# A one-core hybrid attention layer: x normed before it is split, instead of a factor on every projection

## The chip, the cores and the metric

One Trainium2 chip, one of its cores. The metric is device microseconds (us) of one execution of the kernel. All data are float32; matrix products run on float32 values that are first split into a high part `hi` and a remainder `lo`.

## What is computed

The reference, cut to what matters here (S = 256 tokens, width 2048, 256 memory tokens):

```python
h = rmsnorm(x, norm_g)                 # x * rsqrt(mean(x*x)) * norm_g
z = h @ w_in                           # (256, 6144), split into the next line
q_a, k_a, v_a, g_a, u_p, g_p, q_m, g_m = jnp.split(z, IN_OFFSETS, axis=-1)
y_a = causal_attention(q_a, k_a, v_a) * silu(g_a)      # 8 heads x 128
y_p = multiscale_pool(u_p, w_pool, pool_scale) * silu(g_p)
mk, mv = jnp.split(rmsnorm(mem, mem_norm_g) @ w_mem_kv, 2, axis=-1)
y_m = memory_attention(q_m, mk, mv) * silu(g_m)        # 4 heads x 128
y = jnp.concatenate([y_a, y_p, y_m], axis=-1) @ w_out
return rmsnorm(x + y, final_norm_g)
```

## The kernel before

All weights together are 18 **groups** of 512 columns, and a group is 8 **pieces** of 2 x 128 rows (512 KB), so that `n` runs over 144 pieces and `g, a = divmod(n, 8)`. The groups are, in order: MK (n 0 to 7) and MV (8 to 15), the memory's keys and values; Q0 (16 to 23), Q1, K0, K1, V0, V1, GA0, GA1, U, GP, QM, GM, which are projections of x; and four output groups. Every engine runs its own program over the same `n`, and semaphores join them:

- **SP** sends the weights into 8 buffers `w_raw`. In its loop at L276 it waits until piece a of MK has been split, sends piece a of MV (L278) and then two of the 16 slices of x turned (`x_t_raw`, L279). After it `w_pool` and the weights of `w_in` (L285) follow in one queue.
- **ACT** (ScalarE) makes `hi` of piece n+4 in step n (`split_hi`, L516 to L524). That waits for piece n to be used up by TensorE and for piece n+4 to have landed.
- **DVE** (VectorE) makes `lo = raw - hi` of the same piece (`split_lo`, L696).
- **PE** (TensorE) multiplies piece n once `lo` of it is there (L473). Groups MK, Q, K, GA, U, GP, QM, GM go through `rows_are_features` (the wide `hi` product and a half-wide `lo` product), MV, V0, V1 and the output groups through `rows_are_tokens` (three wide products, L387 to L389).
- Results leave PSUM at a == 7: ACT copies one half into `part_b` (L618), DVE adds the other in `evacuate` (L755); V0 and V1 leave with a factor (L746).

The norm of x: x turned is multiplied by `norm_g` alone while it is split, by `x_to_hi` on ACT (L552) and `x_to_lo` on DVE (L724), in steps n = 10 to 17 (`X_FIRST` = 10). The factor 1/rms comes in later. x by rows (`rows`, 2 x 1 MB) is sent from ACT's queue at n == 8 (L630) and squared in steps 16 to 19 (`square_rows`, L535, by the table `SQUARE_STEPS`, L61). At n == 20 DVE takes the mean (`mean_square`, L701), GpSimd raises it to the power -1/2 (L322), and DVE puts it on diagonals (`spread_diag`, L732). After piece n == 22 PE spreads these over all partitions (`spread_rstd`, L348, called at L485), and DVE copies the result to `x_rstd` (L833). All groups of x except Q0, Q1 and QM are then multiplied by `x_rstd` as they leave (L759) or by the token's factor (L746), and the scores' factor is applied in `scale_max` (L762) and in the exponential's scale (L570). In each step of DVE's program the order is: evacuation, `x_rstd`, `split_lo`, the part of x, the mean (L825 to L847). In ACT's: `part_b`, `split_hi`, squares, the DMAs of `rows`, x (L612 to L634).

Of the kernel before, what the change touches and what calls it, by code (L numbers as in the profile page):

```python
# [21 lines left out]
F32 = mybir.dt.float32  # L22
F32R = mybir.dt.float32r
ALU = mybir.AluOpType
ACT = mybir.ActivationFunctionType
AX = mybir.AxisListType

P = 128
D = 2048
S = 256  # L30
# [5 lines left out]
TH = S // P  # L36
# [21 lines left out]
JOBS = (V1, GA0, GM)  # L58
FACTOR = {Q0: SCALE, Q1: SCALE, QM: SCALE, GA0: 0.5, GA1: 0.5, GP: 0.5, GM: 0.5}
BRANCHES = (V1, GA0, GP, GM)  # L60
SQUARE_STEPS = {16: (0,), 17: (1,), 18: (2,), 19: (3,), 24: (4,), 25: (5,), 26: (6,), 27: (7,)}  # L61
X_FIRST = PPG + 2
X_GAIN, POOL_SCALE = 0, KT
X_MEAN, X_SPREAD = 20, 22
GATES = (GA0, GA1, GP, GM)


def build(nc, x, mem, x_t, mem_head, columns, w_in, w_mem_kv, w_pool, w_out, final_g, out):
    with ExitStack() as ctx:
# [3 lines left out]
        def sem(name):  # L73
            return ctx.enter_context(nc.semaphore(name))
# [103 lines left out]
        mk_scaled = sem("mk_scaled")  # L178
        mem_hi = sem("mem_hi")
        mem_lo = sem("mem_lo")  # L180
        x_hi = sem("x_hi")
        x_lo = sem("x_lo")
        mv_scaled = sem("mv_scaled")
# [44 lines left out]
        def bank0(g):  # L228

            return 4 * (g % 2)  # L230
# [18 lines left out]
        @block.sync  # L249
        def _(sp):  # L250
            def mem_slices(i):

                sp.dma_start(mem_raw[:, mem_columns(i)], mem_head[:, mem_columns(i)]).then_inc(mem_landed[i], 16)

            def first_half(a):

                sp.dma_start(w_raw[:, a, 0], kv_dram[0, a, :, 0]).then_inc(first_landed[a], 16)

            def second_half(a):

                sp.dma_start(w_raw[:, a, 1], kv_dram[0, a, :, 1]).then_inc(landed[a], 16)

            sp.dma_start(mem_raw[:, 0:KT + S], mem_head[:, 0:KT + S]).then_inc(mem_first_landed, 16)
            second_half(0)
            mem_slices(1)
            first_half(1)
            second_half(1)
            mem_slices(2)
            first_half(2)
            second_half(2)  # L270
            for a in range(HALVED, PPG):
                if TPP * a in MEM_CHUNKS:
                    mem_slices(MEM_CHUNKS.index(TPP * a))
                sp.dma_start(w_raw[:, a], kv_dram[0, a]).then_inc(landed[a], 16)
            sp.dma_start(cols[:, :], columns).then_inc(cols_landed, 16)
            for a in range(PPG):  # L276
                sp.wait_ge(lo_done, a + 1)
                sp.dma_start(w_raw[:, a], kv_dram[1, a]).then_inc(landed[a], 16)  # L278
                sp.dma_start(x_t_raw[:, TPP * a:TPP * (a + 1)], x_t[:, TPP * a:TPP * (a + 1)]  # L279
                             ).then_inc(x_landed[a], 16)  # L280
            sp.dma_start(wp[:, :, :], w_pool).then_inc(wp_landed, 16)
            with sp.Fori(0, OUT0 - Q0) as g:
                for a in range(PPG):
                    sp.wait_ge(lo_done, g * PPG + (PPG + a + 1))
                    sp.dma_start(w_raw[:, a], in_dram[bass.ds(g, 1), a].rearrange("g p t c -> p (g t) c")  # L285
                                 ).then_inc(landed[a], 16)
            with sp.Fori(0, GROUPS - OUT0) as g:
                for a in range(PPG):
                    sp.wait_ge(lo_done, g * PPG + ((OUT0 - 1) * PPG + a + 1))
                    sp.dma_start(w_raw[:, a], out_w_dram[bass.ds(g, 1), a].rearrange("g p t c -> p (g t) c")  # L290
                                 ).then_inc(landed[a], 16)
            for h in range(TH):
                for i in range(3):
                    c = slice(i * COLS, (i + 1) * COLS)
                    sp.wait_ge(finished_dve, 3 * h + i + 1)
                    sp.dma_start(out_dram[h, :, c], x_res[:, h, c]).then_inc(stored, 16)
                sp.wait_ge(finished_act, h + 1)
                sp.dma_start(out_dram[h, :, D - COLS:], end_scaled[:, h]).then_inc(stored, 16)
            sp.wait_ge(stored, 16 * 4 * TH)
# [215 lines left out]
        def _(act):  # L515
# [35 lines left out]

            def x_to_hi(b):  # L552

                act.wait_ge(x_landed[b], 16)
                for kt in (2 * b, 2 * b + 1):
                    m = act.activation(xT[:, kt, 0], x_t_raw[:, kt], ACT.Copy,
                                       scale=cols[:, X_GAIN + kt:X_GAIN + kt + 1])
                m.then_inc(x_hi, 1)

            def exps(g, pair):  # L560
                j = 2 * JOBS.index(g) + pair
                act.wait_ge(max_ready, j + 1)
                if j == 0:
                    act.wait_ge(mk_scaled, 1)
                for f in range(2 * pair, 2 * pair + 2):
                    for h in range(TH):
                        c, w = (h * M, M) if g == MEM_JOB else (h * P, P + h * P)
                        dst = probs_end if g == MEM_JOB else probs
                        m = act.activation(dst[:, f, c:c + w], ps[:, bank0(g + 1) + f, c:c + w], ACT.Exp,
                                           scale=rstd_in[:, 0, h:h + 1],  # L570
                                           bias=nmax[:, f, h:h + 1], accum_out=sums[:, f, h:h + 1])
                m.then_inc(exp_done, 1)

# [36 lines left out]
            for n in range(PIECES):  # L610
# [14 lines left out]
                    split_hi(m)  # L625
                for k in SQUARE_STEPS.get(n, ()):
                    square_rows(k)
                if n == PPG:
                    for h in range(TH):
                        act.dma_start(rows[:, h], x_dram[h]).then_inc(rows_landed[h], 16)  # L630
                if n == X_FIRST:
                    act.wait_ge(cols_landed, 16)
                if X_FIRST <= n < X_FIRST + PPG:
                    x_to_hi(n - X_FIRST)  # L634
                if n == 20:
# [51 lines left out]
        def _(dve):  # L687
            steps = [0]

            def settle(ins):  # L690

                steps[0] += 1
                ins.then_inc(dve_self, 1)
                dve.wait_ge(dve_self, steps[0])
# [21 lines left out]
            def mem_to_lo(kts):  # L716
                for kt in kts:
# [3 lines left out]
                                             in1=memT[:, kt, 0].bitcast(F32),  # L721
                                             op0=ALU.mult, op1=ALU.subtract).then_inc(mem_lo, 1)

            def x_to_lo(b):  # L724
                dve.wait_ge(x_hi, b + 1)
                for kt in (2 * b, 2 * b + 1):
                    m = dve.scalar_tensor_tensor(out=xT[:, kt, 1], in0=x_t_raw[:, kt],
                                                 scalar=cols[:, X_GAIN + kt:X_GAIN + kt + 1],
                                                 in1=xT[:, kt, 0].bitcast(F32), op0=ALU.mult, op1=ALU.subtract)
                m.then_inc(x_lo, 1)  # L730

            def spread_diag(i):  # L732
                dve.wait_ge(rstd_ready, i + 1)
# [4 lines left out]
            def evacuate(g):  # L738
# [3 lines left out]
                    return  # L742
                if g in TOKENS_ON_ROWS:
                    dst = {V0: v[:, :, 0:COLS], V1: v[:, :, COLS:]}[g]
                    for h in range(TH):
                        m = dve.tensor_scalar(dst[:, h], ps[:, bank0(g) + h, :], rstd_in[:, 0, h:h + 1], None, ALU.mult)  # L746
                    m.then_inc(evacuated, 1)
                    return
                dst = {MK: mkT, QM: qmT, Q0: qT[:, 0:NF], Q1: qT[:, NF:], K0: kT[:, 0:NF], K1: kT[:, NF:],
                       U: u_pad[:, :, PAD:]}.get(g, gate)  # L750
# [1 line left out]
                if g in GATES and g != GA0:  # L752
                    dve.wait_ge(y_lo, GATES.index(g))
                hi_part = ps[:, bank0(g):bank0(g) + NF, 0:S]
                m = dve.scalar_tensor_tensor(out=dst[:, :, :], in0=hi_part, scalar=FACTOR.get(g, 1.0),  # L755
                                             in1=part_b[:, :, :], op0=ALU.mult, op1=ALU.add)
                if g not in (MK, Q0, Q1, QM):
                    settle(m)
                    m = dve.tensor_tensor(dst[:, :, :], dst[:, :, :], x_rstd[:, :, :].to_broadcast([P, NF, S]), ALU.mult)  # L759
                m.then_inc(evacuated, 1)  # L760

            def scale_max(own):  # L762

                dve.tensor_tensor(nmax[:, own, :], nmax[:, own, :], rstd_in[:, 0:1, :].to_broadcast([P, 2, TH]),
                                  ALU.mult).then_inc(max_ready, 1)

            def mask_and_max(g, pair):
                j = 2 * JOBS.index(g) + pair
# [1 line left out]
                b = bank0(g + 1) + 2 * pair  # L770
                own = slice(2 * pair, 2 * pair + 2)
                if g == MEM_JOB:
                    settle(dve.tensor_reduce(nmax[:, own, :], ps[:, b:b + 2, :].rearrange("p f (h k) -> p f h k", h=TH),
                                             AX.X, ALU.max, negate=True))
                    scale_max(own)
                    return

                diag = ps[:, b:b + 2, :].rearrange("p f (h k) -> p f h k", h=TH)[:, :, :, 0:P]
                settle(dve.tensor_tensor(diag, diag, mask[:, :].rearrange("p (f h k) -> p f h k", f=1, h=1)
                                         .to_broadcast([P, 2, TH, P]), ALU.add))  # L780
                dve.tensor_reduce(nmax[:, own, 0:1], ps[:, b:b + 2, 0:P], AX.X, ALU.max, negate=True)
                settle(dve.tensor_reduce(nmax[:, own, 1:2], ps[:, b:b + 2, P:P + S], AX.X, ALU.max, negate=True))
                scale_max(own)

            def normalise(g, pair):
                j = 2 * JOBS.index(g) + pair
# [37 lines left out]
            for n in range(PIECES):  # L824
# [13 lines left out]
                    split_lo(m)  # L838
                if n == X_FIRST:
                    dve.wait_ge(cols_landed, 16)  # L840
                if X_FIRST <= n < X_FIRST + PPG:
                    x_to_lo(n - X_FIRST)
                if n == X_MEAN:
                    mean_square(0)
# [97 lines left out]
```

## Time and profile before

| | us |
|---|---|
| median of 3 runs | 440.05 (439.99 to 440.51) |
| the profiled execution's own time | 439.82 |
| its span, first to last instruction | 437.6 |
| PE busy | 428.5 |
| DVE busy | 266.3 |
| ACT busy | 220.1 |
| GpSimd busy | 26.5 |

The span is 2.2 us shorter than the execution's time. Rows of a timeline are: start, duration, engine, line, operation, output and inputs, count, and in brackets the idle time before it with what ended it. "PE" is the matmul, "PEld" the load of its stationary operand, which overlaps. Matmul rows overlap each other, since their ends are modelled.

### The profile page before, as it was taken

How to read it: one execution, taken by the hardware profiler on the slowest of the kernel's cores; microseconds unless marked ns; L12 is line 12 of the kernel's file. 1: busy time of each engine (PE TensorE's matmuls, PEld its weight loads, DVE VectorE, ACT ScalarE, POOL GpSimd, SP SyncE). 2: the span in 40 equal slices, each digit the busy share in tenths (PEclk: the TensorE clock that was granted, in tenths of full speed). 3: DMA queues.
4: the chain of work that ended last, by engine and by line, in shares of the span. 5: the costliest groups of instructions: out<-in, count | busy, mean ns of one | idle time of the engine just before them, and what ended most of it. 6: DMA issues, size and time to landing. Idle time of an engine off the chain costs nothing.

```text
span 437.6 us, 6006 instructions
## 1 busy us (share of the span) xinstructions
PE 428.5 (98%) x2252; PEld 367.8 (84%) x2252; DVE 266.3 (61%) x293; ACT 220.1 (50%) x298; POOL 26.5 (6%) x48
## 2 busy tenths in 40 slices
PE   9999999999999999999999999999999999999992
PEld 8888888888888888888988888888888888888881
DVE  4865865545464685746466767848663674648522
ACT  6854784743444435536545444454465544357311
POOL 1000000000000020000020200010000202020200
PEclk9999999999999999999999999999999999999998
DMA  8999969655556554643629866445735256746022
GB/s 286 405 402 411 389 197 381 193 187 183 190 176 193 188 169 161 189 145 99 194 97 355 318 202 199 160 168 185 219 119 192 95 175 212 228 156 194 0 97 97
DMA packets 25657, 89.77 MB, mean 205 GB/s; under 512 B 2976, under 2 KB 3232, under 8 KB 24736
## 3 DMA queue, kind: packets, MB, share of 16 engines
q1 hardware_dynamic: 24336, 81.69, 54.9%
q10 hardware_dynamic: 1296, 7.73, 4.3%
q8 instruction: 18, 0.29, 0.3%
q14 instruction: 7, 0.06, 0.1%
HBM read 87.31 MB, written 2.10 MB: 204 GB/s over the span
## 4 chain that ended last, share of the span: by engine, by line
PE 95%; issue 2%; DVE 0%; POOL 0%; ACT 0%; POOLq 0%; DVEq 0%
PE ps L365 38%; PE ps L368 17%; PE ps L387 11%; PE ps L389 11%; PE ps L388 11%; PE ps L374 1%; PE ps L444 1%; PE ps L404 1%; PE ps L435 1%; PE ps L431 1%; PE ps L399 1%; PE ps L419 1%; PE ps L403 0%; PE ps L436 0%; PE ps L415 0%
## 5 line engine op out<-in xcount | busy, mean ns | idle before, releaser
L699 DVE TENSOR_TENSOR w_lo<-w_raw,w_hi 128x1024 fp32r<-128x1024 f32 x137 | 173.9, 1282 | 119.4 <-ACT w_hi L524 119.0
L524 ACT ACTIVATE w_hi<-w_raw 128x1024 fp32r<-128x1024 f32 x137 | 143.7, 1058 | 130.1 <-PE ps L368 74.6
L365 PE MATMUL ps<-xT,w_hi 128*128 128x512 f32 x640 | 200.6, 397 | 0.0
L368 PEld LDWEIGHTS ps<-xT,w_lo 128*128 128x128 f32 x600 | 112.7, 188 | 26.6
L368 PE MATMUL ps<-xT,w_lo 128*128 128x256 f32 x600 | 118.1, 278 | 0.0
L365 PEld LDWEIGHTS ps<-xT,w_hi 128*128 128x128 f32 x640 | 98.8, 189 | 1.3
L387 PE MATMUL ps<-w_hi,yT 128*128 128x512 f32 x112 | 43.6, 389 | 0.0
L388 PE MATMUL ps<-w_lo,yT 128*128 128x512 f32 x112 | 43.6, 389 | 0.0
L389 PE MATMUL ps<-w_hi,yT 128*128 128x512 f32 x112 | 43.6, 389 | 0.0
L387 PE MATMUL ps<-w_hi,xT 128*128 128x512 f32 x64 | 25.5, 399 | 0.0
L389 PE MATMUL ps<-w_hi,xT 128*128 128x512 f32 x64 | 25.0, 390 | 0.0
L388 PE MATMUL ps<-w_lo,xT 128*128 128x512 f32 x64 | 24.9, 389 | 0.0
L389 PEld LDWEIGHTS ps<-w_hi,yT 128*128 128x128 f32 x112 | 21.0, 188 | 4.4
L388 PEld LDWEIGHTS ps<-w_lo,yT 128*128 128x128 f32 x112 | 21.0, 188 | 4.4
L387 PEld LDWEIGHTS ps<-w_hi,yT 128*128 128x128 f32 x112 | 21.0, 188 | 4.3
L618 ACT ACTIVATE part_b<-ps 128x1024 f32<-128x1024 f32 x11 | 11.3, 1027 | 20.3 <-PE ps L368 20.3
L365 PE MATMUL ps<-memT,w_hi 128*128 128x512 f32 x64 | 20.6, 407 | 0.0
L333 POOL TENSOR_TENSOR gate<-gate,att 128x1024 f32<-128x1024 f32 x4 | 9.6, 2411 | 122.0 <-ACT part_b L666 122.0
L595 ACT ACTIVATE squares<-x_res 128x512 f32<-128x512 f32 x8 | 5.1, 633 | 22.5 <-DVE x_res L891 15.2
L389 PEld LDWEIGHTS ps<-w_hi,xT 128*128 128x128 f32 x64 | 12.0, 188 | 2.6
L388 PEld LDWEIGHTS ps<-w_lo,xT 128*128 128x128 f32 x64 | 12.0, 188 | 2.3
L387 PEld LDWEIGHTS ps<-w_hi,xT 128*128 128x128 f32 x64 | 12.0, 188 | 2.3
(129 smaller groups left out, 384.9 us busy)
## 6 DMA issues: line engine op xcount, KB each, us to landing
w_raw<-in_w_in SPq DMA_DIRECT2D x96, 512.0 KB, 4.2
w_raw<-in_w_out SPq DMA_DIRECT2D x32, 512.0 KB, 4.2
w_raw<-in_w_mem_kv SPq DMA_DIRECT2D x13, 512.0 KB, 13.1
x_t_raw<-in_x_t SPq DMA_DIRECT2D x8, 256.0 KB, 13.6
rows<-in_x ACTq DMA_DIRECT2D x2, 1024.0 KB, 10.5
rows<-in_mem ACTq DMA_DIRECT2D x2, 1024.0 KB, 9.0
x_res<-in_x ACTq DMA_DIRECT2D x2, 1024.0 KB, 8.9
mem_raw<-in_mem_head SPq DMA_DIRECT2D x3, 512.0 KB, 7.6
```

What stands on the lines that cost most here:

```text
L333: pool.tensor_tensor(gate[:, :, :], gate[:, :, :], att[:, i % 2], ALU.mult).then_inc(gate_att, 1)
L365: pe.matmul(ps[:, bank0(g) + f, :], hi[:, t, f * P:(f + 1) * P], moving[:, kt], start=(kt == 0), stop=(kt == KT - 1), skip_group_check=True)
L368: m = pe.matmul(ps[:, bank0(g) + f, 0:S], lo[:, t, f * P:(f + 1) * P], moving[:, kt, 0], start=False, stop=(kt == KT - 1), skip_group_chec ...
L374: pe.matmul(ps[:, bank0(g) + f, 0:S], lo[:, t, f * P:(f + 1) * P], moving[:, kt, 0], start=False, stop=False, skip_group_check=True)
L387: pe.matmul(acc, stationary[:, kt, 0, tok], hi[:, t, :], start=(kt == 0), stop=False)
L388: pe.matmul(acc, stationary[:, kt, 0, tok], lo[:, t, :], start=False, stop=False)
L389: m = pe.matmul(acc, stationary[:, kt, 1, tok], hi[:, t, :], start=False, stop=(kt == KT - 1))
L399: m = pe.matmul(ps[:, b, h * M:(h + 1) * M], qmT[:, f, h * P:(h + 1) * P], mkT[:, f, :], start=True, stop=True)
L524: act.activation(halves_of(n)[0], w_raw[:, n % RAW], ACT.Copy).then_inc(hi_done, 1)
L595: act.activation(squares[:, 0:c.stop - c.start], x_res[:, h, c], ACT.Square, scale=D ** -0.5, accum_out=ssq[:, h, i:i + 1]).then_inc(sq_do ...
L618: act.activation(part_b[:, :, :], ps[:, bank0(g):bank0(g) + NF, S:2 * S], ACT.Copy, scale=FACTOR.get(g, 1.0)).then_inc(part_b_ready, 1)
L699: dve.tensor_tensor(lo, w_raw[:, n % RAW], hi.bitcast(F32), ALU.subtract).then_inc(lo_done, 1)
```

## The change

x turned is multiplied in place by `norm_g` and 1/rms on DVE (`norm_x`), one step ahead of its use, and only then split: ACT copies two slices in one instruction, DVE subtracts in one. For this `x_rstd` has to be known before the split. Its mean moves from step 20 to step 10, the spreading from 22 to 12, the squares from steps 16 to 19 to steps 6 to 9, and the split of x from steps 10 to 17 to steps 13 to 20. x by rows is sent by SP, half 0 behind piece 0 of MV's weights and slices of x, half 1 behind piece 1. The factors at the exits are gone.

```diff
-SQUARE_STEPS = {16: (0,), 17: (1,), 18: (2,), 19: (3,), 24: (4,), ...}
-X_FIRST = PPG + 2
+SQUARE_STEPS = {6: (0,), 7: (1,), 8: (2,), 9: (3,), 24: (4,), ...}
+X_MEAN, X_SPREAD = PPG + 2, PPG + 4
+X_FIRST = X_SPREAD + 1
-X_MEAN, X_SPREAD = 20, 22
@@ SP, after piece a of MV and its slices of x_t
+                if a < TH:
+                    sp.dma_start(rows[:, a], x_dram[a]).then_inc(rows_landed[a], 16)
@@ ACT
             def x_to_hi(b):
-                act.wait_ge(x_landed[b], 16)
-                for kt in (2 * b, 2 * b + 1):
-                    m = act.activation(xT[:, kt, 0], x_t_raw[:, kt], ACT.Copy,
-                                       scale=cols[:, X_GAIN + kt:X_GAIN + kt + 1])
-                m.then_inc(x_hi, 1)
+                act.wait_ge(x_normed, b + 1)
+                act.activation(xT[:, 2 * b:2 * b + 2, 0], x_t_raw[:, 2 * b:2 * b + 2], ACT.Copy).then_inc(x_hi, 1)
@@ exps
-                                           scale=rstd_in[:, 0, h:h + 1],
@@ ACT's loop
-                if n == PPG:
-                    for h in range(TH):
-                        act.dma_start(rows[:, h], x_dram[h]).then_inc(rows_landed[h], 16)
-                if n == X_FIRST:
-                    act.wait_ge(cols_landed, 16)
@@ DVE
+            def norm_x(b):
+                dve.wait_ge(x_landed[b], 16)
+                for kt in (2 * b, 2 * b + 1):
+                    m = dve.scalar_tensor_tensor(out=x_t_raw[:, kt], in0=x_t_raw[:, kt],
+                                                 scalar=cols[:, X_GAIN + kt:X_GAIN + kt + 1],
+                                                 in1=x_rstd[:, 0, :], op0=ALU.mult, op1=ALU.mult)
+                m.then_inc(x_normed, 1)
             def x_to_lo(b):
+                own = slice(2 * b, 2 * b + 2)
                 dve.wait_ge(x_hi, b + 1)
-                for kt in (2 * b, 2 * b + 1):
-                    m = dve.scalar_tensor_tensor(out=xT[:, kt, 1], in0=x_t_raw[:, kt], ...)
-                m.then_inc(x_lo, 1)
+                dve.tensor_tensor(xT[:, own, 1], x_t_raw[:, own], xT[:, own, 0].bitcast(F32), ALU.subtract
+                                  ).then_inc(x_lo, 1)
@@ evacuate: V0, V1
-                    for h in range(TH):
-                        m = dve.tensor_scalar(dst[:, h], ps[:, bank0(g) + h, :], rstd_in[:, 0, h:h + 1], None, ALU.mult)
+                    dve.tensor_copy(dst, ps[:, bank0(g):bank0(g) + TH, :]).then_inc(evacuated, 1)
@@ evacuate: the others keep the scalar_tensor_tensor alone
-                if g not in (MK, Q0, Q1, QM):
-                    settle(m)
-                    m = dve.tensor_tensor(dst[:, :, :], dst[:, :, :], x_rstd[:, :, :].to_broadcast([P, NF, S]), ALU.mult)
@@ mask_and_max: scale_max and the settle ahead of it are gone
-            def scale_max(own):
-                dve.tensor_tensor(nmax[:, own, :], nmax[:, own, :], rstd_in[:, 0:1, :].to_broadcast([P, 2, TH]),
-                                  ALU.mult).then_inc(max_ready, 1)
@@ DVE's loop
                 if n == X_FIRST:
                     dve.wait_ge(cols_landed, 16)
+                    norm_x(0)
                 if X_FIRST <= n < X_FIRST + PPG:
+                    if n + 1 < X_FIRST + PPG:
+                        norm_x(n + 1 - X_FIRST)
                     x_to_lo(n - X_FIRST)
```

## Rows read from the trace of the kernel before

**Rows 1.** The page: busy time by engine, and GB/s moved in 40 slices of the span.
```profile
PE 428.5 (98%) x2252; PEld 367.8 (84%) x2252; DVE 266.3 (61%) x293; ACT 220.1 (50%) x298; POOL 26.5 (6%) x48
...
GB/s 286 405 402 411 389 197 381 193 187 183 190 176 193 188 169 161 189 145 99 194 97 355 318 202 199 160 168 185 219 119 192 95 175 212 228 156 194 0 97 97
```
**Rows 2.** Stretches: length, busy PE, PEld, DVE, ACT, POOL, granted clock, DMA share, GB/s.
```profile
6.70:429.50 422.80, 422.76 (x2230) 362.26 (x2228) 261.73 (x284) 214.94 (x289) 23.94 (x17) 1.00 0.60 207
429.60:433.20 3.60, 0.00 (x0) 0.00 (x0) 2.82 (x6) 1.45 (x3) 0.55 (x1) 1.00 0.00 0
433.40:437.60 4.20, 0.00 (x0) 0.00 (x0) 0.00 (x0) 0.00 (x0) 0.00 (x0) 0.50 0.74 239
```
**Rows 3.** The chain that ended last: shares by engine, then three of its pieces.
```profile
PE 95%; issue 2%; DVE 0%; POOL 0%; ACT 0%; POOLq 0%; DVEq 0%
...
1.00 4.63 PE ps L444 x20
5.63 1.49 PE ps L365 x4
...
51.27 0.92 PE ps L365 x4
```
**Rows 4.** Groups of DVE instructions by line and shape: busy us, mean ns, idle before.
```profile
L759 DVE TENSOR_TENSOR gate<-gate,x_rstd 128x1024 f32<-128x1024 f32 x4 | 4.9, 1226 | 0.1
...
L746 DVE TENSOR_SCALAR v<-ps,rstd_in 128x512 f32<-128x512 f32 x4 | 2.8, 746 | 2.1 <-PE ps L389 2.1
...
L709 DVE TENSOR_TENSOR w_lo<-w_raw,w_hi 128x512 fp32r<-128x512 f32 x3 | 2.1, 693 | 0.5 <-ACT w_hi L530 0.5
...
L764 DVE TENSOR_TENSOR nmax<-nmax,rstd_in 128x4 f32<-128x4 f32 x6 | 1.0, 163 | 0.2
```
**Rows 5.** SP's queue, 10 to 12.2 us: DMA issues.
```profile
10.06 0.59 SPq L278 DMA_DIRECT2D w_raw<-in_w_mem_kv  x1
...
12.17 0.68 SPq L278 DMA_DIRECT2D w_raw<-in_w_mem_kv  x1
```
**Rows 6.** DMA issues from 12.0 to 12.2 us: size, us from issue to landing.
```profile
w_raw<-in_w_mem_kv SPq DMA_DIRECT2D x1, 512.0 KB, 13.9
```
**Rows 7.** ACT's timeline, 26 to 42 us.
```profile
26.19 1.06 ACT L524 ACTIVATE w_hi<-w_raw 128x1024 fp32r<-128x1024 f32 x1 [0.89 <-PE ps L368]
28.91 1.02 ACT L618 ACTIVATE part_b<-ps 128x1024 f32<-128x1024 f32 x1 [1.67 <-PE ps L368]
29.84 1.05 ACT L524 ACTIVATE w_hi<-w_raw 128x1024 fp32r<-128x1024 f32 x1
...
37.31 1.06 ACT L524 ACTIVATE w_hi<-w_raw 128x1024 fp32r<-128x1024 f32 x1 [1.74 <-PE ps L389]
...
40.11 1.06 ACT L524 ACTIVATE w_hi<-w_raw 128x1024 fp32r<-128x1024 f32 x1 [0.94 <-PE ps L389]
```
**Rows 8.** ACT's timeline, 54 to 71 us.
```profile
54.11 1.06 ACT L524 ACTIVATE w_hi<-w_raw 128x1024 fp32r<-128x1024 f32 x1 [0.95 <-PE ps L368]
55.08 1.04 ACT L540 ACTIVATE rows<-rows 128x1024 f32<-128x1024 f32 x1
...
56.12 0.89 ACT L556 ACTIVATE xT<-x_t_raw,cols 128x256 fp32r<-128x256 f32 x2
...
65.26 1.06 ACT L524 ACTIVATE w_hi<-w_raw 128x1024 fp32r<-128x1024 f32 x1 [0.69 <-PE ps L368]
...
70.83 1.06 ACT L524 ACTIVATE w_hi<-w_raw 128x1024 fp32r<-128x1024 f32 x1 [1.73 <-PE ps L368]
```
**Rows 9.** DVE's timeline, the diagonals of 1/rms.
```profile
68.67 0.48 DVE L735 TENSOR_SCALAR diag<-ident,rstd_in 128x128 f32<-128x128 f32 x2 [0.83 <-POOL rstd_in L322]
```
**Rows 10.** PE's timeline around the spreading of 1/rms.
```profile
70.64 0.60 PE L351 MATMUL ps<-diag,ones 128*128 128x128 f32 x4
71.00 0.70 PE L365 MATMUL ps<-xT,w_hi 128*128 128x512 f32 x2
```
**Rows 11.** DVE's timeline, 50 to 53 us.
```profile
50.74 0.88 DVE L727 SCALAR_TENSOR_TENSOR xT<-x_t_raw,cols,xT 128x256 fp32r<-128x256 f32 x2
51.53 1.22 DVE L741 COPY mv<-ps 128x1024 f32<-128x1024 f32 x1
52.67 1.22 DVE L699 TENSOR_TENSOR w_lo<-w_raw,w_hi 128x1024 fp32r<-128x1024 f32 x1
```

More of the change, by code:

```diff
@@ L60 @@
 BRANCHES = (V1, GA0, GP, GM)
-SQUARE_STEPS = {16: (0,), 17: (1,), 18: (2,), 19: (3,), 24: (4,), 25: (5,), 26: (6,), 27: (7,)}
-X_FIRST = PPG + 2
+SQUARE_STEPS = {6: (0,), 7: (1,), 8: (2,), 9: (3,), 24: (4,), 25: (5,), 26: (6,), 27: (7,)}
+X_MEAN, X_SPREAD = PPG + 2, PPG + 4
+X_FIRST = X_SPREAD + 1
 X_GAIN, POOL_SCALE = 0, KT
-X_MEAN, X_SPREAD = 20, 22
 GATES = (GA0, GA1, GP, GM)
@@ L180, in build @@
         mem_lo = sem("mem_lo")
+        x_normed = sem("x_normed")
         x_hi = sem("x_hi")
@@ L722, in mem_to_lo @@
                                              op0=ALU.mult, op1=ALU.subtract).then_inc(mem_lo, 1)
+            def norm_x(b):
[5 more added lines that the diff above has]
+                m.then_inc(x_normed, 1)
             def x_to_lo(b):
+                own = slice(2 * b, 2 * b + 2)
                 dve.wait_ge(x_hi, b + 1)
-                for kt in (2 * b, 2 * b + 1):
-                    m = dve.scalar_tensor_tensor(out=xT[:, kt, 1], in0=x_t_raw[:, kt],
-                                                 scalar=cols[:, X_GAIN + kt:X_GAIN + kt + 1],
-                                                 in1=xT[:, kt, 0].bitcast(F32), op0=ALU.mult, op1=ALU.subtract)
-                m.then_inc(x_lo, 1)
+                dve.tensor_tensor(xT[:, own, 1], x_t_raw[:, own], xT[:, own, 0].bitcast(F32), ALU.subtract
+                                  ).then_inc(x_lo, 1)
             def spread_diag(i):
@@ L744, in evacuate @@
                     dst = {V0: v[:, :, 0:COLS], V1: v[:, :, COLS:]}[g]
-                    for h in range(TH):
-                        m = dve.tensor_scalar(dst[:, h], ps[:, bank0(g) + h, :], rstd_in[:, 0, h:h + 1], None, ALU.mult)
-                    m.then_inc(evacuated, 1)
+                    dve.tensor_copy(dst, ps[:, bank0(g):bank0(g) + TH, :]).then_inc(evacuated, 1)
                     return
@@ L754, in evacuate @@
                 hi_part = ps[:, bank0(g):bank0(g) + NF, 0:S]
-                m = dve.scalar_tensor_tensor(out=dst[:, :, :], in0=hi_part, scalar=FACTOR.get(g, 1.0),
-                                             in1=part_b[:, :, :], op0=ALU.mult, op1=ALU.add)
-                if g not in (MK, Q0, Q1, QM):
-                    settle(m)
-                    m = dve.tensor_tensor(dst[:, :, :], dst[:, :, :], x_rstd[:, :, :].to_broadcast([P, NF, S]), ALU.mult)
-                m.then_inc(evacuated, 1)
-            def scale_max(own):
-                dve.tensor_tensor(nmax[:, own, :], nmax[:, own, :], rstd_in[:, 0:1, :].to_broadcast([P, 2, TH]),
-                                  ALU.mult).then_inc(max_ready, 1)
+                dve.scalar_tensor_tensor(out=dst[:, :, :], in0=hi_part, scalar=FACTOR.get(g, 1.0),
+                                         in1=part_b[:, :, :], op0=ALU.mult, op1=ALU.add).then_inc(evacuated, 1)
             def mask_and_max(g, pair):
@@ L772, in mask_and_max @@
                 if g == MEM_JOB:
-                    settle(dve.tensor_reduce(nmax[:, own, :], ps[:, b:b + 2, :].rearrange("p f (h k) -> p f h k", h=TH),
-                                             AX.X, ALU.max, negate=True))
-                    scale_max(own)
+                    dve.tensor_reduce(nmax[:, own, :], ps[:, b:b + 2, :].rearrange("p f (h k) -> p f h k", h=TH),
+                                      AX.X, ALU.max, negate=True).then_inc(max_ready, 1)
                     return
@@ L781, in mask_and_max @@
                 dve.tensor_reduce(nmax[:, own, 0:1], ps[:, b:b + 2, 0:P], AX.X, ALU.max, negate=True)
-                settle(dve.tensor_reduce(nmax[:, own, 1:2], ps[:, b:b + 2, P:P + S], AX.X, ALU.max, negate=True))
-                scale_max(own)
+                dve.tensor_reduce(nmax[:, own, 1:2], ps[:, b:b + 2, P:P + S], AX.X, ALU.max, negate=True
+                                  ).then_inc(max_ready, 1)
             def normalise(g, pair):
```

## The prediction

> **What bounds the kernel now.** I read the page first. PE is busy 428.5 us, all but 9 us of the span, while DVE and ACT have 40% and 50% of it free [rows 1]. Then the stretches: from 6.70 to 429.50 us PE is idle for 0.04 us in all, at a granted clock of 1.00, that is 2.4 GHz [rows 2]. So PE waits for nobody from its second piece to its last, and the chain that ended last is 95% PE [rows 3]. Two readings follow. Work taken from DVE or ACT buys nothing, because no matmul waits for them. And a wait of PE that the change makes is not absorbed anywhere: all later work moves by it, one for one. What is left outside PE, 1 us at the start and 8 us behind the last matmul (the norm and the stores of the last group), has no line of the diff in it. The question is only whether something now arrives late.
>
> **What is removed.** DVE loses seven multiplications by `x_rstd` at the exits (four of them the gate row, 1.23 us each, the others alike), six `scale_max` of 0.16 us, and the four `tensor_scalar` of V0 and V1 (0.75 us each) become two copies of 1.22 us like that of `mv` [rows 4, 11]. That is some 10 us of DVE time, and the ends of the chains that lead to scores and gates come about 1.2 us earlier. I cost this at nothing: the cover is PE's own work, and PE reaches every one of these waits with the semaphore already up [rows 2]. The exponential without a scale vector is the same instruction. ACT loses the issue of two DMAs, which ran in idle time.
>
> **What is moved: the rows of x.** SP now puts 2 x 1.05 MB into its own queue, ahead of the issues at 10.06 and at 12.17 us [rows 5]. Those two issues themselves cost SP about 0.5 us each and hide, since its transfers already stand some 14 us in line: the one issued at 12.17 lands 13.9 us later, at 26.1 [rows 5, 6]. That one is piece 2 of MV, n = 10, and it is exactly the one that ACT picks up at 26.19 [rows 7]. The DMAs run at capacity there, 402 to 411 GB/s in the slices from 11 to 55 us [rows 1]. A queue served in order therefore hands piece 10 over 2.1 MB / 0.402 = 5.2 us later, at 31.3. Piece 9 comes 2.6 us later and has time. Both halves of the rows land ahead of piece 10, so the squares never wait for data. From 31.3 on, weights come every 0.79 MB / 0.402 = 1.96 us, and what followed the rows in the old order is neither earlier nor later than before, because the same bytes stand ahead of it: piece 16 still comes at about 43.5.
>
> **What that does to ACT.** From 31.4 us ACT has no pause for ten instructions: `hi` of piece 10, square 0, `part_b` of MK, `hi` 11, square 1, `hi` 12, square 2, `hi` 13, square 3, `hi` 14. From start to start a `hi` ahead of a square takes 0.97 us, a square with its read-out 1.04 [rows 8], `part_b` 0.93 [rows 7]. The sum is 4 x 0.97 + 4 x 1.04 + 0.93 + 1.06 (the last `hi` in full) = 10.0, so `hi` 14 ends at 41.4. Before, it would have ended at 38.4 (37.31 + 1.06) [rows 7]. The weights are no longer what ACT waits for by then: piece 14 lands at 31.3 + 4 x 1.96 = 39.1, and its turn comes at 40.4. On the way PE gets piece 11 with 0.3 us to spare: `part_b` ends at 34.4, the exit of MK on DVE at 35.6, `lo` 11 at 36.9, and PE wants it at 37.1 (ACT saw piece 10 used at 37.31 [rows 7], PE is free 0.19 earlier, as below).
>
> **The wait that opens.** DVE takes the mean only after `lo` 14. In the trace the same sequence stands ten steps later: `hi` 24 starts at 65.26 and ends at 66.32 [rows 8], then `lo` 24, the sums, the power on GpSimd (0.83 of waiting) and the diagonals, which end at 68.67 + 0.48 = 69.15 [rows 9]: 2.83 us behind the `hi`. So the diagonals of x are ready at 41.4 + 2.8 = 44.2. PE wants them when piece 12 is through. ACT would see piece 11 used at 40.11 [rows 7] and piece 12 one pace of 2.80 later, at 42.91; PE itself goes on 0.19 earlier (it began the spreading at 70.64 where ACT's `hi` began at 70.83 [rows 8, 10]), at 42.7. PE stands from 42.7 to 44.2, and I add 0.1 for the way through the semaphore: **1.6 us**. In the old place the same wait had 70.64 - 69.15 = 1.5 us to spare; it lost 3 us. Its bounds are 0, if the rows hold nothing up, and 2.9, if the transfers come another 1.3 us late (the rows' two halves would need 6.5 us, 323 GB/s, between the saturated 402 and the mean of a light slice near 190). I take 1.6, which goes by the saturated slices [rows 1], the ones that the transfer is in. The spreading matmuls themselves, 0.36 us [rows 10], were there before.
>
> **What it does to the split of x.** Per step DVE now has `lo` (1.14 from start to start), `norm_x` (two 128x256 instructions; no row has this operation, but the shape, the operands and the opcode are those of the old split, 0.79 for two from 50.74 to 51.53) and one subtraction of 128x512, of which a row gives 0.69 in full, 0.61 from start to start [rows 4, 11]. That makes 2.54 against PE's 2.80 a piece. The bounds for it are 2.54 and, if nothing overlaps, 1.22 + 0.96 + 0.69 = 2.87. With the stall, PE starts piece 13 at 44.7 and piece 14 at 47.5. ACT's `hi` 17 ends at 48.7, `lo` 17 at 49.9, two `norm_x` at 51.5, x 0 at 52.2, wanted at 53.1. ACT turns to `hi` 18 only when the first x is rounded, so it ends at 52.5 and x 1 comes at 55.1 (wanted 55.9). Then the exit of MV stands ahead (1.14 [rows 11]) and x 2 comes at 58.8, wanted at 58.7. I take a second stall of **0.15 us**; behind it DVE gains a quarter of a microsecond per step. `x_rstd` itself is copied at 45.5, under `lo` 15 and 16, whose pieces are wanted at 50 and later.
>
> **Sum.** 439.82 (the profiled execution) + 1.6 + 0.15 = 441.6. The median shown, 440.05, is 0.23 above that execution, so against the median it is 1.5 to 1.8 us, 0.4%. About 0.2%, 0.9 us, is what a measurement of this kernel can tell from no change.
>
> **Rivals.** *The rows hold nothing up* (not slower): piece 10 lands by 29.7, 1.6 us sooner than I have it. That is the point that decides: then ACT's ten instructions end by 39.8, the diagonals are there at 42.6, and the second stall goes too: 439.9. For it: the margins are all of one microsecond, and the transfers might be interleaved in another way than strictly in line. Against it: the DMAs are saturated in these slices [rows 1], bytes put ahead must be paid, and a landing time of 13.9 us at the issue of 12.17 is what a queue served in order gives [rows 5, 6]. Chance 0.20.
> *The new DVE work becomes the bound* (slower still): a step costs 2.87 instead of 2.54. Then x 2 comes 0.33 later for each of three steps, and the five steps after it lose 0.07 each instead of gaining: 0.15 + 1.0 + 0.3 = 1.4 us in place of 0.15, together 442.9. Against it: instructions of this kind follow each other 0.09 us sooner than their lengths say, wherever they stand back to back [rows 11]. Chance 0.15.
> *The clock falls in the stall.* In this trace PE was never idle for long between its pieces, so no row shows what 1.6 us do. Behind the last matmul PE is idle from 429.6 to 433.2 with the clock still granted at 1.00, and only after that does it show 0.50, the level of 1.2 GHz [rows 2]. At the start PE ran from 1.00, and its first four wide matmuls took 1.49 us from 5.63 where four take 0.92 later [rows 3], so the low level lasted some 5.6 us. That again would lose 2.8: 444.4. [...] Chance 0.04.
> *Faster*: PE's pace itself would have to rise with less traffic from DVE. Nothing in the rows does so; chance 0.03, about 439.
>
> **How the numbers follow.** My forecast has 0.58. The range 439.9 to 443.0 takes in the forecast with its bounds, the first rival down to its value and the second; left out are the clock, the faster case and part of the first rival. Slower by more than 0.2%: 0.58 + 0.15 + 0.04, less a little for stalls that come out under 0.9 us, 0.75. Faster 0.03, the rest, 0.22, within 0.2%.
>
> **What the profile after would show.** Right: a gap of PE of 1 to 2 us ahead of L351 at about 43 us, ended by DVE's `diag`; ACT waiting for the DMA of `w_raw` until about 31.3 and then without a pause until 41; DVE nearly full from 48 to 70; nothing else of PE's idle changed, and every later stage shifted by one constant. Wrong: no gap at L351 (the rows held nothing up), a gap ahead of piece 10 or 11 (the transfers came later than 31.6), gaps of PE in Q0 of over 0.3 us each (DVE is the bound), or a granted clock under 1.00 behind 44 us.

## The result, and the profile after

The changed kernel takes 441.69 us (median of 7 runs, 441.36 to 441.81) against 440.05 us before (7 runs, 439.72 to 440.51). The ratio is 1.0036, 95% interval 1.0027 to 1.0046: slower by 1.6 us. The forecast was 441.6, in a range of 439.9 to 443.0.

The profiled execution of the changed kernel has a time of 441.81 us and a span of 439.5 us, 1.9 us more than that of before. The page after, and its chain that ended last:

```profile
PE 428.5 (97%) x2252; PEld 366.8 (83%) x2252; DVE 261.3 (59%) x286; ACT 216.4 (49%) x290; POOL 26.5 (6%) x48
...
GB/s 279 409 407 404 345 191 319 258 189 190 191 192 192 186 152 191 176 128 126 193 98 373 296 212 194 152 181 179 193 140 187 97 194 189 222 160 192 1 97 96
...
PE 86%; DMA 5%; ACT 3%; issue 3%; DVE 1%; SPq 1%; POOL 0%; POOLq 0%; DVEq 0%; ACTq 0%
PE ps L368 34%; PE ps L371 16%; PE ps L390 10%; PE ps L391 10%; PE ps L392 10%; DMA w_raw<-in_w_mem_kv 5%; ACT w_hi L527 1%; PE ps L377 1%; ACT rows L543 1%; PE ps L407 1%; PE ps L438 1%; PE ps L434 1%; PE ps L402 1%; PE ps L422 1%; DVE w_lo L693 0%
```

PE's busy time is what it was [rows 1], and DVE has lost 5 us, net of the new `norm_x`. What has changed is the chain: before it was 95% PE [rows 3], now 5% of it are a DMA of the memory's weights and 3% ACT, with the squares' line in it. So for a stretch the end hangs on a transfer. The waits of PE of the changed kernel (us in total, times, longest):

```profile
PE ps L354 <- DVE diag L735: 1.1, 1, 1.1
PE ps L447 <- POOL ones L307: 1.0, 1, 1.0
PE ps L368 <- DVE w_lo L707: 0.4, 1, 0.4
PE ps L368 <- DVE memT L713: 0.3, 1, 0.3
```

The one that matters is new, the spreading matmul waiting for the diagonals. The other three lie in the first 8 us; the one of 1.0 is in the kernel before too. PE's timeline around it:

```profile
42.73 0.39 PE L392 MATMUL ps<-w_hi,memT 128*128 128x512 f32 x1
44.24 0.71 PE L354 MATMUL ps<-diag,ones 128*128 128x128 f32 x4 [1.12 <-DVE diag L735]
44.71 0.48 PE L390 MATMUL ps<-w_hi,memT 128*128 128x512 f32 x1
```

The view's idle time is 1.12 us because it counts from the modelled end of the last matmul. At its pace of 0.23 us PE could have gone on at 42.96, so it stood for 1.28, and the spreading took 0.47 instead of 0.36 [rows 10]: the wait costs 1.4 us. What lies ahead of it, on SP's queue:

```profile
9.50 0.44 SPq L280 DMA_DIRECT2D x_t_raw<-in_x_t  x1
9.98 0.90 SPq L283 DMA_DIRECT2D rows<-in_x  x1
10.92 1.05 SPq L279 DMA_DIRECT2D w_raw<-in_w_mem_kv  x1
12.01 1.05 SPq L280 DMA_DIRECT2D x_t_raw<-in_x_t  x1
13.11 1.05 SPq L283 DMA_DIRECT2D rows<-in_x  x1
14.20 1.07 SPq L279 DMA_DIRECT2D w_raw<-in_w_mem_kv  x1
```

The last of these is piece 10. It lands 17.1 us after its issue:

```profile
w_raw<-in_w_mem_kv SPq DMA_DIRECT2D x1, 512.0 KB, 17.1
```

That is at 31.3, where it was 26.1 before [rows 5, 6]. And ACT's timeline from there, which shows pieces 9 and 10 waited for, and then ten instructions without a pause:

```profile
26.97 1.06 ACT L527 ACTIVATE w_hi<-w_raw 128x1024 fp32r<-128x1024 f32 x1 [3.96 <-DMA w_raw<-in_w_mem_kv]
31.42 1.06 ACT L527 ACTIVATE w_hi<-w_raw 128x1024 fp32r<-128x1024 f32 x1 [3.39 <-DMA w_raw<-in_w_mem_kv]
32.39 1.05 ACT L543 ACTIVATE rows<-rows 128x1024 f32<-128x1024 f32 x1
...
33.43 1.00 ACT L617 ACTIVATE part_b<-ps 128x1024 f32<-128x1024 f32 x1
34.33 1.05 ACT L527 ACTIVATE w_hi<-w_raw 128x1024 fp32r<-128x1024 f32 x1
...
40.30 2.00 ACT L527 ACTIVATE w_hi<-w_raw 128x1024 fp32r<-128x1024 f32 x2
```

On DVE the mean follows `lo` 14, and the diagonals end at 44.18:

```profile
41.38 1.23 DVE L693 TENSOR_TENSOR w_lo<-w_raw,w_hi 128x1024 fp32r<-128x1024 f32 x1 [0.76 <-ACT w_hi L527]
...
43.70 0.48 DVE L735 TENSOR_SCALAR diag<-ident,rstd_in 128x128 f32<-128x128 f32 x2 [0.83 <-POOL rstd_in L325]
...
55.08 1.22 DVE L741 COPY mv<-ps 128x1024 f32<-128x1024 f32 x1
56.22 1.22 DVE L693 TENSOR_TENSOR w_lo<-w_raw,w_hi 128x1024 fp32r<-128x1024 f32 x1
57.35 0.88 DVE L721 SCALAR_TENSOR_TENSOR x_t_raw<-x_t_raw,cols,x_rstd 128x256 f32<-128x256 f32 x2
58.14 0.69 DVE L729 TENSOR_TENSOR xT<-x_t_raw,xT 128x512 fp32r<-128x512 f32 x1
```

The last four rows are step 15. x 2 is ready at 58.83, and PE wanted it a little earlier. That second stall is too short to be listed as a wait, because modelled ends of matmuls cover it. PE's own rows show it, at the start of piece 18:

```profile
58.06 0.63 PE L368 MATMUL ps<-xT,w_hi 128*128 128x512 f32 x2
58.53 0.39 PE L371 MATMUL ps<-xT,w_lo 128*128 128x256 f32 x2
58.89 0.73 PE L368 MATMUL ps<-xT,w_hi 128*128 128x512 f32 x2
59.46 0.39 PE L371 MATMUL ps<-xT,w_lo 128*128 128x256 f32 x2
```

The two `lo` products of a pair take 0.23 us elsewhere in this stretch, so PE could have gone on at 58.76; it started at 58.89, and the next pair took 0.57 where 0.47 is usual: 0.23 us in all. The same shows in the pace at which ACT finds pieces used:

```profile
56.17 1.06 ACT L527 ACTIVATE w_hi<-w_raw 128x1024 fp32r<-128x1024 f32 x1 [0.94 <-PE ps L371]
...
58.96 1.06 ACT L527 ACTIVATE w_hi<-w_raw 128x1024 fp32r<-128x1024 f32 x1
...
61.98 1.06 ACT L527 ACTIVATE w_hi<-w_raw 128x1024 fp32r<-128x1024 f32 x1 [0.55 <-PE ps L371]
```

These rows are 2.79 us apart between the first two and 3.02 between the next two: 0.23 us. The stretches of the changed kernel, with the columns of [rows 2]:

```profile
7.20:42.80 35.60, 35.20 (x180) 29.57 (x180) 24.00 (x34) 25.47 (x39) 0.00 (x0) 1.00 1.03 405
45.00:431.20 386.20, 386.20 (x2040) 331.28 (x2038) 231.01 (x241) 184.61 (x241) 23.25 (x16) 1.00 0.56 186
```

From 45.00 us on, the second stall included, no idle time of PE is listed, and the granted clock is 1.00 as before. It is 1.00 over the first stall too (42.80 to 45.00). The shift of the last matmul between the two traces is 1.87 us (429.19 to 431.06). It is made of 1.4, of 0.23, and of 0.25 by which ACT's `hi` 3 starts later already (12.05 and 12.30), whose piece is issued ahead of the first edit in SP's program. The last part differs from one execution to the next: in the ten traces of the changed kernel and its variants below, `hi` 3 starts between 12.14 and 12.47, and at 12.20 in the old kernel of experiment 1. The medians, 1.64 apart, agree with 1.4 and 0.23 alone.

### The profile page after: what moved, and what is told of

It reads as the page before. It is cut to its first block, busy times and chain, and to the rows that moved or that the text cites. A ratio compares the mean times of both kernels' runs of the same rounds, so it can differ in the third digit from the quotient of the medians.

```text
span 439.5 us, 5990 instructions
## 1 busy us (share of the span) xinstructions
PE 428.5 (97%) x2252; PEld 366.8 (83%) x2252; DVE 261.3 (59%) x286; ACT 216.4 (49%) x290; POOL 26.5 (6%) x48
## 4 chain that ended last, share of the span: by engine, by line
PE 86%; DMA 5%; ACT 3%; issue 3%; DVE 1%; SPq 1%; POOL 0%; POOLq 0%; DVEq 0%; ACTq 0%
PE ps L368 34%; PE ps L371 16%; PE ps L390 10%; PE ps L391 10%; PE ps L392 10%; DMA w_raw<-in_w_mem_kv 5%; ACT w_hi L527 1%; PE ps L377 1%; ACT rows L543 1%; PE ps L407 1%; PE ps L438 1%; PE ps L434 1%; PE ps L402 1%; PE ps L422 1%; DVE w_lo L693 0%
```

## The experiments

Each kernel below was timed beside the kernel before. Its time is the median of 5 to 11 executions, and the ratio is to the kernel before, with its 95% interval.

**1. Two parts of the change in the old kernel.** x by rows on SP's queue and the squares early, everything else as before.

```diff
-SQUARE_STEPS = {16: (0,), 17: (1,), 18: (2,), 19: (3,), ...}
+SQUARE_STEPS = {6: (0,), 7: (1,), 8: (2,), 9: (3,), ...}
@@ SP, behind piece a of MV and its slices
+                if a < TH:
+                    sp.dma_start(rows[:, a], x_dram[a]).then_inc(rows_landed[a], 16)
@@ ACT's loop
-                if n == PPG:
-                    for h in range(TH):
-                        act.dma_start(rows[:, h], x_dram[h]).then_inc(rows_landed[h], 16)
```

> The kernel before with two parts of the change alone: x by rows on SP's queue behind pieces 0 and 1 of MV, and the squares in steps 6 to 9. Mean, spreading, split of x and exits as before. Theory A: the transfers are late by 5.2 us as in the changed kernel (ACT waits until 31.4 for piece 10), but PE never waits, because lo 10 and lo 11 still come in time: 440.05, ratio 1.000. Rival E (the late pieces themselves stall PE, the mean only follows): a gap of PE around 34 to 38 us, up to 1.6 us, 441.0 to 441.7.

Measured: 440.01 us, ratio 1.000 (0.9991 to 1.0009). ACT waits for piece 10 as in the changed kernel:

```profile
31.10 1.06 ACT L526 ACTIVATE w_hi<-w_raw 128x1024 fp32r<-128x1024 f32 x1 [3.38 <-DMA w_raw<-in_w_mem_kv]
```

PE has no wait but the one at its start. Late pieces and early squares, together, cost nothing, so what costs is that something is wanted of ACT's late chain by piece 12.

**2. The rows spread out.** Halves behind pieces 1 and 3.

```diff
-                if a < TH:
-                    sp.dma_start(rows[:, a], x_dram[a]).then_inc(rows_landed[a], 16)
+                if a in (1, 3):
+                    sp.dma_start(rows[:, a // 2], x_dram[a // 2]).then_inc(rows_landed[a // 2], 16)
```

> The changed kernel, but the halves of x by rows are sent behind pieces 1 and 3 of MV instead of 0 and 1. Theory A (the first stall comes from ACT's chain of ten instructions, which starts when piece 10 lands): piece 10 lands at 28.7 us, the last piece that the mean waits for (n = 14) still at 39.1, hi 14 ends at 40.4, the diagonals at 43.2, so the gap ahead of L354 shrinks from 1.12 us shown (1.4 in cost) to some 0.3 to 0.5; time 440.6, ratio to before 1.001. Rival B (the gap has nothing to do with the order of the transfers, PE would wait for the mean wherever they stand): gap unchanged, 441.7.

Measured: 440.78 us, ratio 1.0017 (1.0007 to 1.0026), 0.9 under the changed kernel's first median. ACT picks up piece 10 at 28.61, the diagonals end at 42.93, and no wait of PE is listed at L354. The direction and nearly the size are theory A's. The gap came out smaller in the profile than expected, though the time is 0.2 above the expectation. The last matmul starts 0.61 later than in the trace of before, and that is 0.22 at piece 18, 0.20 around the spreading (0.09 ahead of it, 0.11 in it, none of it listed as a wait) and 0.20 by which `hi` 3 starts later (12.25 for 12.05). The medians are 0.81 apart, and the two stalls explain 0.42 of that; the rest stays open.

**3. The mean ahead of `lo` 14.**

```diff
+                if n == X_MEAN:
+                    mean_square(0)
+                    spread_diag(0)
                 for m in pieces_to_split(n):
                     split_lo(m)
-                if n == X_MEAN:
-                    mean_square(0)
-                    spread_diag(0)
```

> The changed kernel, but DVE takes the mean and makes the diagonals ahead of lo 14 in step 10 instead of behind it. Theory A: the diagonals need only square 3, which ends at 40.4; they are ready at 42.0 to 42.2, before PE wants them at 42.7 to 43.0. No gap ahead of L354, only the second stall of 0.22 us in Q0 stays: 440.3 (ratio 1.0005). Rival C (the gap is the length of the norm's chain over three engines as such, not its place behind lo 14): moving it gains at most the 1.1 us of lo 14 if ACT's hi 14 was not what it waited for, gap of 0.3 or more left, 440.6 or more.

Measured: 440.38 us, ratio 1.0012 (1.0003 to 1.0021). The diagonals of this kernel:

```profile
41.78 0.48 DVE L735 TENSOR_SCALAR diag<-ident,rstd_in 128x128 f32<-128x128 f32 x2 [0.83 <-POOL rstd_in L325]
42.18 2.36 DVE L693 TENSOR_TENSOR w_lo<-w_raw,w_hi 128x1024 fp32r<-128x1024 f32 x2
```

They end at 42.26, and PE starts the spreading at 42.87 without a wait, although piece 10 was as late as ever (31.49). What is left is the second stall, 0.25 in this trace (`hi` 21 at 57.49, `hi` 22 at 60.53). Rival C falls: what stalls PE is not the length of the norm's chain, but its place behind `hi` 14 and `lo` 14.

**4. The same, and the first two `norm_x` a step earlier.**

```diff
-                if n == X_FIRST:
+                if n == X_SPREAD:
                     dve.wait_ge(cols_landed, 16)
                     norm_x(0)
+                    norm_x(1)
                 if X_FIRST <= n < X_FIRST + PPG:
-                    if n + 1 < X_FIRST + PPG:
+                    if X_FIRST < n < X_FIRST + PPG - 1:
                         norm_x(n + 1 - X_FIRST)
```

> As the kernel with the mean first, and also the first two norm_x move from step 13 to step 12, behind lo 16, where DVE stands idle for 2 us. Theory A: the second stall (x 2 wanted at piece 18) goes as well, PE without a gap from piece 1 on: 440.05, the time of before, within 0.1. Rival D (DVE is the bound in Q0 however the steps are placed, since it is nearly full there): the shift of 0.2 us or more in Q0 stays, 440.3.

Measured: 440.06 us, ratio 1.000 (0.9991 to 1.0009). The pace at piece 18 is 2.78 again (`hi` 21 at 57.47, `hi` 22 at 60.25). Two rearrangements on DVE give back what the change cost, within the 0.1% of the interval, with every transfer where the change put it. It is not faster than the kernel before: the rearranged kernel leaves PE as dense as the old one, and no wait is left that could be removed that way.

**5. The changed kernel itself,** timed again beside the kernels of experiments 6 and 9 and the second run of experiment 7.

> The changed kernel itself, unedited, so that the others of this call stand beside it on the same chip. All theories: 441.4 to 441.8, ratio 1.0036; the gap ahead of L354 is 0.7 to 1.2 us, according to when piece 10 lands in the profiled execution (30.9 to 31.5 us so far).

Measured: 441.53 us, ratio 1.0033 (1.0021 to 1.0045), gap 1.1 us, piece 10 picked up at 31.24.

**6. `norm_x` earlier alone.** The diff of experiment 4 in the changed kernel, with the mean where the change has it.

> The changed kernel with the first two norm_x in step 12 instead of 13, the mean where the change has it (behind lo 14). Theory A: the first stall stays as it is, the second of 0.2 in Q0 goes: 0.2 under the changed kernel, 441.4. Rival D (one wait only, the second is a tail of the first): same time as the changed kernel, and hi 22 on ACT still 0.2 later against hi 21.

Measured: 441.21 us, ratio 1.0027 (1.0017 to 1.0038), 0.32 under the changed kernel of experiment 5. In its trace the first stall is there (0.7 us listed) and the second is not (2.79 from `hi` 21 at 58.57 to `hi` 22 at 61.36). Part of the shorter first stall is that PE came to it 0.21 later here than in experiment 5, and part that piece 10 was picked up 0.23 earlier (31.01). The intervals of the two times overlap, so the separation of the stalls rests on the traces.

**7. The factors back at the exits.** The seven multiplications of `x_rstd` behind K, GA, U, GP and GM stand in the changed kernel again (so these groups carry 1/rms twice). `m` is the addition ahead of the lines shown.

```diff
+                if g not in (MK, Q0, Q1, QM):
+                    settle(m)
+                    m = dve.tensor_tensor(dst[:, :, :], dst[:, :, :], x_rstd[:, :, :].to_broadcast([P, NF, S]), ALU.mult)
+                m.then_inc(evacuated, 1)
```

> The changed kernel with the seven multiplications by x_rstd put back at the exits of K, GA, U, GP and GM (the factor then stands twice in these groups; all other work is the same). Theory A (work of DVE behind the projections is covered by PE): 441.7, the changed kernel's time within 0.2, with DVE 8.6 us busier. Rival F (the shorter exits gained something that hid part of the stalls): slower than the changed kernel by 0.5 us or more, 442.2.

Measured: 441.23 us, ratio 1.0029 (1.0018 to 1.0041). This is 0.46 under the changed kernel's first median, so it was timed once more beside it:

> The kernel with the seven multiplications back, once more beside the changed kernel on one chip (its first value, 441.23, lay 0.46 under the changed kernel's from another call). Theory A (exits are covered): within 0.2 of the changed kernel of this call. Rival I (the extra work at the exits makes it faster by 0.4): 0.4 under it again.

Measured: 441.43 us, ratio 1.0033 (1.0021 to 1.0045), against 441.53 of the changed kernel. DVE is 8 us busier in it, and nothing is lost or won:

```profile
PE 427.8 (97%) x2252; PEld 366.5 (83%) x2252; DVE 269.2 (61%) x293; ACT 215.8 (49%) x290; POOL 26.5 (6%) x48
```

The first difference goes with the landing of piece 10 in the two profiled executions, picked up at 30.94 here and at 31.42 in the first one of the changed kernel; the listed gaps were 0.7 and 1.1. Whether it lands earlier in the other executions too, and why, is not shown.

**8. The mean one step later.**

```diff
-                if n == X_MEAN:
+                if n == X_MEAN + 1:
```

> The changed kernel with the mean and the diagonals one step later (step 11, behind lo 15). Theory A (a PE wait in MV is paid one for one and the clock stays): the diagonals come at 45.3 to 45.4 instead of 44.2, the gap ahead of L354 grows by 1.1 to 1.2 us, the total by the same: 442.9, granted clock 1.00 throughout. Rival G (the longer idle stretch of 2.3 to 2.6 us lowers the clock): 444 or more, with a stretch at 0.50 in the records. Rival H (part of the wait is absorbed later): under 442.3.

Measured: 442.88 us, ratio 1.0073 (1.0059 to 1.0087). PE's wait, and the stretch behind it:

```profile
PE ps L354 <- DVE diag L735: 1.8, 1, 1.8
```
```profile
46.00:431.90 385.90, 385.90 (x2039) 331.22 (x2038) 230.54 (x240) 184.37 (x240) 23.23 (x16) 1.00 0.55 185
```

An idle stretch of 1.8 us leaves the granted clock at 1.00, in it (43.00 to 45.10) and behind it. The gap grew by 1.1 us against the kernel with the factors back, timed beside it, and by 0.7 against the first trace of the changed kernel, where piece 10 came 0.27 later. Nothing is absorbed: the last matmul starts 1.34 later than in the kernel with the factors back (431.91 and 430.57), which is the 1.1 and the 0.24 by which `hi` 3 starts later. The median is the 442.9 expected, but the profiled execution (442.63) had a shorter gap than the 2.2 to 2.3 of the expectation, since the diagonals were there at 45.04 and not at 45.3. What a stretch longer than this does to the clock between matmuls is not shown.

**9. One more megabyte in the queue.** A third transfer of 1 MB behind the second half of the rows, into a buffer that is free then. ACT waits for it before that buffer's first use (not shown below).

```diff
+                if a == 1:
+                    sp.dma_start(att[:, :, :, :].rearrange("p i f c -> p (i f c)"), x_dram[0]).then_inc(extra_landed, 16)
```

> The changed kernel with one more transfer of 1 MB (a half of x by rows into a buffer that is free then) behind half 1 of the rows in SP's queue. Theory A (piece 10 pays for every byte put ahead of it, and the diagonals follow it): piece 10 is picked up at 33.6 to 34.1, PE waits some 1.5 us for lo 10 and the rest ahead of L354, and the total is 2.6 us above the changed kernel: 444.3. Rival B (the transfers are not what the chain hangs on): under 442.5. Rival J (queue not served in order, the extra transfer takes its turn beside the weights): piece 10 picked up before 33, 442.5 to 443.5.

Measured: 443.96 us, ratio 1.0088 (1.0074 to 1.0101), 2.43 above the changed kernel of experiment 5. Piece 10 is picked up 2.34 us later, and PE waits twice:

```profile
33.58 1.06 ACT L530 ACTIVATE w_hi<-w_raw 128x1024 fp32r<-128x1024 f32 x1 [5.91 <-DMA w_raw<-in_w_mem_kv]
```
```profile
PE ps L357 <- DVE diag L740: 1.4, 1, 1.4
PE ps L393 <- DVE w_lo L698: 1.3, 1, 1.3
```

Rival J falls: the queue handed on its bytes as if in order, and what was put ahead of piece 10 was paid by PE.

## Why the prediction was right

**The bound.** Right. PE was dense from its second piece on [rows 2], so work taken from DVE bought nothing: with 8 us of it put back the time was the same (experiment 7). And a wait opened in the middle stayed to the end (experiments 8 and 9).

**Removed work at nothing.** Right, by experiment 7 for the seven multiplications. The two copies for V0 and V1 and the missing `scale_max` were not tried alone.

**The rows' transfer.** Piece 10 was forecast at 31.3 and landed at 31.3; over the profiled executions with the rows in this place ACT picked it up between 30.94 and 31.49. Small points: the prediction gave the slices from 11 to 55 us 402 to 411 GB/s, but that holds to 44 us only, and the slice behind shows 389 [rows 1]; the landing of piece 10 lies in the part where it holds. SP took 0.90 and 1.05 us to issue the halves, not 0.5, which hid as forecast. The third megabyte of experiment 9 cost 2.3 to 2.4 us and not the 2.6 expected from 402 GB/s. Piece 16 was forecast at 43.5 and ACT took it up at 44.15 (43.59 before), ahead of PE's need for it.

**ACT's chain.** Forecast: ten instructions from 31.4, `hi` 14 done at 41.4. In the trace `hi` 14 starts at 40.30 and DVE takes up `lo` 14 at 41.38. That neither the late transfers nor the early squares hurt by themselves, only the early use of the mean, is experiment 1. That `lo` 14 stood needlessly in the way is experiment 3. How much of ACT's full stretch comes from the four squares and how much from the late landing was not separated: experiment 2 moves the landing alone, and no run moves the squares alone.

**The first stall.** Forecast 1.6, measured 1.4. The diagonals were there at 44.18 as forecast (44.2), but PE was ready for them at 42.96 instead of 42.7, and `hi` 3 had started 0.25 later in that execution. A chain that hangs on a transfer doesn't shift with PE, so the stall was shorter by that much. The sum of 0.1 for the restart was a little low: the way through the semaphore took 0.06 (44.18 to 44.24), and the spreading, which the prediction left at its old 0.36, took 0.11 more.

**The second stall.** Forecast 0.15, measured 0.23, with x 2 ready at 58.83 (58.8) and wanted at 58.76 (58.7); the rest is 0.06 from `x` 2 to the matmul and 0.10 for the slower pair that starts there. It went away with two `norm_x` in an idle place (experiments 4 and 6), and `norm_x` had the price of the old instruction of its shape (0.88 for two).

**The sum.** 1.75 was forecast over the profiled execution; the medians differ by 1.64, and by 1.46 in experiment 5. That 441.6 and 441.69 agree to 0.1 is partly chance: the sum starts from the profiled execution of before, 0.23 under its median, and from the median it would give 441.8. Of the rivals, "the rows hold nothing up" falls with the landing of piece 10. "DVE is the bound" falls with steps of 2.52 us in the trace (56.22 to 58.74 and on), and "faster" with the ratio. The clock stays at 1.00 in this stall and in the longer one of experiment 8. The price of 2.8 us that the prediction gave it rests on the length of four matmuls at the start; the granted clock is recorded as 1.00 there (0.00 to 5.63 us in the trace of before), so no row shows that low level or its price.

## What to carry to other kernels

Where the matrix engine has no gap, as here, moving work off the other engines is worth nothing (8 us of DVE work put back changed nothing), and the question about a change is which due time it brings forward. When a reduction has to be known earlier, count everything its inputs queue behind: the bytes ahead in the DMA queue, and the weight splits ahead on both other engines. Placed ahead of a split that PE wanted only later, the same mean made PE wait no more, with all transfers unchanged.

## What was not expected of the hardware

With 1.05 MB more in SP's queue the next piece came 2.34 us later, where 402 to 411 GB/s [rows 1] make it 2.6. The transfers weren't faster for that: over the stretch from 22.00 to 33.50 us the trace of experiment 9 shows 411 GB/s, and that of experiment 5 shows 406 from 22.00 to 31.30. The difference lies within the half microsecond by which the pick-up of piece 10 moves from one execution to the next, and its cause was not looked for. A stall of 0.23 us is in no list of waits and can be read only from the starts of the matmuls and the pace of the pieces.
